# The first expert's tokens made by TensorE from the rows in SBUF, instead of gathered from DRAM

## The reference

```python
x = x + gate1 * ((sig(gA) * A @ w_pa + sig(gB) * B @ w_pb) @ w_o)
h = rmsnorm_mod(x, norm2_g, sh2, sc2)
# top-1 of 4 groups, then top-2 of its 4 experts, per token
y = sum over experts e of combine[:, e] * ((silu(h @ w_gate[e]) * (h @ w_up[e])) @ w_down[e])
x = x + gate2 * y
```

## Time and profile before

| | us |
|---|---|
| median of 3 runs | 1282.19 (1280.95 to 1283.69) |
| the profiled execution, its own time | 1284.0 |
| its span, first to last instruction | 1282.3 |
| mean granted TensorE clock | 0.984 |
| busy: PE, DVE, ACT, POOL | 1213.0, 666.9, 541.0, 200.3 |

### The profile page before, as it was taken

How to read it: one execution, slowest core, us unless ns; L and a number is a source line. 1 busy time by engine, 2 the same in 40 slices (tenths; PEclk the granted TensorE clock), 3 DMA queues, 4 the chain that set the end, 5 groups by cost and what they waited for, 6 DMA issues and landing times.

```text
span 1282.3 us, 17725 instructions
## 1 busy us (share of the span) xinstructions
PE 1213.0 (95%) x7058; PEld 923.6 (72%) x7058; DVE 666.9 (52%) x903; ACT 541.0 (42%) x850; POOL 200.3 (16%) x230
## 2 busy tenths in 40 slices
PE   4999999999999999998899999999999999999986
PEld 2677877777777987896766666657667887777762
DVE  2428433222162213213577641354777988888867
ACT  4533322111273135216333332121547777877742
POOL 2113200020000010002200021000163222323230
PEclk9999999999999999998899999999989999999999
DMA  9653222274534452557799995621689999999963
GB/s 335 245 214 108 81 66 66 66 240 146 215 117 130 172 208 105 180 190 263 274 347 384 380 332 193 203 107 33 218 278 321 378 373 375 370 373 378 372 229 119
DMA packets 128922, 294.47 MB, mean 230 GB/s; under 512 B 10016, under 2 KB 10144, under 8 KB 125080
## 3 DMA queue, kind: packets, MB, share of 16 engines
q1 hardware_dynamic: 111112, 243.57, 54.0%
q0 software_dynamic: 17744, 49.96, 11.0%
HBM read 270.44 MB, written 30.42 MB: 235 GB/s over the span
## 4 chain that ended last, share of the span: by engine, by line
PE 67%; DMA 19%; issue 4%; ACT 3%; DVE 3%; POOL 3%; POOLq 1%; SPq 0%; ACTq 0%; DVEq 0%
PE psum L1040 14%; PE psum L1042 14%; PE psum L1041 14%; DMA arena<-slots_d 9%; PE psum L1028 5%; PE psum L1102 5%; DMA arena<-in_cache_kv_w_dram 5%; DMA arena<-h2d,arena 3%; PE psum L1449 2%; PE psum L1283 2%; PE psum L1356 2%; PE psum L1055 1%; POOL slots_d L958 1%; POOL arena L977 1%; ACT arena L1665 1%
## 5 line engine op out<-in xcount | busy, mean ns | idle before, releaser
L1040 PE MATMUL psum<-part,part 128*128 128x512 f32 (+1 forms) x1088 | 437.0, 402 | 6.0 <-DVE part L2545 2.3
L1041 PE MATMUL psum<-part,part 128*128 128x512 f32 (+1 forms) x1088 | 428.9, 394 | 0.0
L1042 PE MATMUL psum<-part,part 128*128 128x512 f32 (+1 forms) x1088 | 428.6, 394 | 0.0
L1040 PEld LDWEIGHTS psum<-part,part 128*128 128x128 f32 (+1 forms) x1088 | 219.4, 202 | 61.2 <-issue 13.7
L1042 PEld LDWEIGHTS psum<-part,part 128*128 128x128 f32 (+1 forms) x1088 | 219.4, 202 | 42.6
L1041 PEld LDWEIGHTS psum<-part,part 128*128 128x128 f32 (+1 forms) x1088 | 219.6, 202 | 38.5
L2505 DVE TENSOR_TENSOR part<-arena,part 128x2048 fp32r<-128x2048 f32 x96 | 218.3, 2290 | 34.1 <-ACT part L1900 32.6
L1900 ACT ACTIVATE part<-arena 128x2048 fp32r<-128x2048 f32 x94 | 178.7, 1918 | 36.1 <-DMA arena<-in_w_down_dram 16.4
L1665 ACT ACTIVATE arena<-psum 128x512 f32<-128x512 f32 (+4 forms) x127 | 73.4, 598 | 273.0 <-PE psum L1042 223.3
L1999 DVE TENSOR_TENSOR part<-arena,part 128x2048 fp32r<-128x2048 f32 x42 | 96.0, 2299 | 141.4 <-PE psum L1102 118.3
L1028 PE MATMUL psum<-cst,arena 128*128 128x128 f32 (+2 forms) x746 | 103.8, 285 | 30.5 <-ACT arena L1693 9.7
(11 more groups left out here) (308 smaller groups left out, 1105.0 us busy)
## 6 DMA issues: line engine op xcount, KB each, us to landing
arena<-in_w_in_dram SPq DMA_DIRECT2D x34, 1024.0 KB, 5.4
arena<-in_cache_kv_w_dram SPq DMA_DIRECT2D x16, 2048.0 KB, 12.2
arena<-in_w_gate_dram SPq DMA_DIRECT2D x32, 1024.0 KB, 9.7
arena<-in_w_up_dram SPq DMA_DIRECT2D x32, 1024.0 KB, 8.9
arena<-in_w_down_dram SPq DMA_DIRECT2D x32, 1024.0 KB, 10.2
arena<-in_w_ada_dram SPq DMA_DIRECT2D x8, 2048.0 KB, 7.7
arena<-in_cache_kv_w_dram SPq DMA_DIRECT2D x16, 1024.0 KB, 9.7
arena<-in_w_ada_dram SPq DMA_DIRECT2D x8, 1024.0 KB, 14.4
```

Source lines behind the costliest of these rows:

```text
L1040: nc.tensor.matmul(out_, hi, w_hi, start=start, stop=False)
L1041: nc.tensor.matmul(out_, hi, w_lo, start=False, stop=False)
L1042: last_product[0] = nc.tensor.matmul(out_, lo, w_hi, start=False, stop=stop)
```

## The change

The gather of expert 0's tokens goes. PE makes them, already turned, into the same banks 0 and 1: for each block of 128 columns of h, the sum over the five tiles of `hrow`'s block (as weights) with `hot[0]`'s tile. POOL gathers for experts 1 and 2 only. `hot[0]` and `xg` lie elsewhere, since `hrow` must now stay until the products are made; SP's second `ahead` load waits for them (`x_filled` 2) too. The orders on PE, ACT and DVE around the change are written anew, and the six keep-warm products that PE makes behind the bank "pos" (two, three and one) go; the six in front of it stay.

```diff
-        hot = [kept[:, a:a + TILES * P].rearrange("p (i n) -> p i n", i=TILES) for a in (0, 3072, 1200)]
+        hot = [[gt_tmp[:, i * P:(i + 1) * P] for i in range(4)] + [at(KEPT0 + 6 * CH + D + 1100, P)]] + [
+            [kept[:, a + i * P:a + (i + 1) * P] for i in range(TILES)] for a in (3072, 1200)]
...
-        xg = at(TAIL0, 2, D)
+        xg = [at(TAIL0 + D, D), at(TAIL0, D)]
...
             sp.wait_ge(h2_out, 16 * TILES)
+            sp.wait_ge(x_filled, 2)
             sp.dma_start(ahead[1], gate1[:, 4:8, :]).then_inc(ahead_in[1], 16)
-            for par in range(2):
-                sp.wait_ge(xg_in[par], 16)
+            sp.wait_ge(xg_in[1], 16)
...
             pool.wait_ge(h2_out, 16 * TILES)
-            for e in range(3):
-                pool.wait_ge(slot_ready, e + 1)
+            pool.dma_start(yd[2 * TOK + 2:2 * TOK + 3, :], h2d[2:3, :]).then_inc(xg_in[0], 16)
+            for e in (1, 2):
+                pool.wait_ge(slot_ready, e)
                 if e == 2:
                     pool.wait_ge(x_filled, 2)
...
             mm.wait_emptied(pe, len(mm.users) - 1)
-            keep_warm(2)
-            for e in range(3):
+            tp.wait_emptied(pe, len(tp.users) - 1)
+            def place_of_slots(e):
                 pe.wait_ge(hot_done, e + 1)
                 for i in range(TILES):
-                    ins = nc.tensor.matmul(psum[:, 2 + e, 0:1], hot[e][0:ROWS[i], i, :], tok_left[0:ROWS[i], i:i + 1],
+                    ins = nc.tensor.matmul(psum[:, 2 + e, 0:1], hot[e][i][0:ROWS[i], :], tok_left[0:ROWS[i], i:i + 1],
                                            start=(i == 0), stop=(i == TILES - 1))
                 ins.then_inc(hot_filled, 1)
-            keep_warm(3)
+            pe.wait_ge(hot_done, 1)
+            for c in range(2):
+                for k in range(4):
+                    if c == 0 and k == 2:
+                        place_of_slots(1)
+                    for i in range(TILES):
+                        n, f = ROWS[i], (4 * c + k) * P
+                        ins = nc.tensor.matmul(psum[:, c, k * P:(k + 1) * P], hrow[0:n, i, f:f + P], hot[0][i][0:n, :],
+                                               start=(i == 0), stop=(i == TILES - 1))
+                ins.then_inc(x_filled, 1)
+            place_of_slots(2)
...
             prime(pe, 1, up_read, up_filled, y0_filled, y1_filled)
-            for c in range(2):
-                turn_tokens(0, 0, 0, c)
-            keep_warm(1)
             pe.wait_ge(x_lo, 1)
...
-            for at_ in range(2, 4):
-                high(at_, 16)
+            high(2, 16)
+            tokens_high(0, 0, 0)
+            high(3, 16)
+            tokens_high(0, 0, 1)
             rounds = rounds_of(act)
-            for c in range(2):
-                tokens_high(0, 0, c)
+            act.wait_ge(h2_out, 16 * TILES)
             silu(0)
...
-            slots_of(0)
+            slots_of(1)
+            low(0, 7)
+            tokens_low(0, 0, 0)
+            low(1, 8)
             compared(2)
-            low(0, 7)
-            slots_of(1)
+            tokens_low(0, 0, 1)
             for k, mk in enumerate((m1, m2)):
...
             V.tensor_copy(row_u, rowf).then_inc(rows_done, 1)
             slots_of(2)
-            low(1, 8)
             rounds = rounds_of(dve)
...
-            for c in range(2):
-                tokens_low(0, 0, c)
             for at_ in range(2, 4):
                 low(at_, at_ + 7)
```

More of the change, by code:

```diff
@@ L947, in _ @@
             pool.wait_ge(h2_out, 16 * TILES)
-            for e in range(3):
-                pool.wait_ge(slot_ready, e + 1)
+            pool.dma_start(yd[2 * TOK + 2:2 * TOK + 3, :], h2d[2:3, :]).then_inc(xg_in[0], 16)
+            for e in (1, 2):
+                pool.wait_ge(slot_ready, e)
                 if e == 2:
                     pool.wait_ge(x_filled, 2)
-                pool.indirect_dma_start(xg[:, e % 2, :], None, h2d, bass.IndirectOffsetOnAxis(
+                pool.indirect_dma_start(xg[e % 2], None, h2d, bass.IndirectOffsetOnAxis(
                     ap=slot_hot[:, e:e + 1], axis=0), bounds_check=TOK - 1, oob_is_err=False).then_inc(xg_in[e % 2], 16)
@@ L976, in fetch @@
                 waited()
-                pool.indirect_dma_start(xg[:, par, :], None, h2d, bass.IndirectOffsetOnAxis(
+                pool.indirect_dma_start(xg[par], None, h2d, bass.IndirectOffsetOnAxis(
                     ap=slot_u[:, par, 0:1], axis=0), bounds_check=TOK - 1, oob_is_err=False).then_inc(xg_in[par], 16)
@@ L1567, in turn_tokens @@
                     pe.wait_ge(xg_in[par], it * 16 + 16)
-                if not isinstance(n, int) or n > 0:
-                    pe.wait_ge(x_lo, n * 2 + c - 1)
+                pe.wait_ge(x_lo, n * 2 + c - 1)
                 for k in range(4):
                     ins = nc.tensor.transpose(X[c][:, k * P:(k + 1) * P],
-                                              xg[:, par, (4 * c + k) * P:(4 * c + k + 1) * P], ident)
+                                              xg[par][:, (4 * c + k) * P:(4 * c + k + 1) * P], ident)
                 ins.then_inc(x_filled, 1)
@@ L2490, in compared @@
                 for i in range(TILES):
-                    ins = V.tensor_scalar(hot[e][:, i, :], c_("iota"), 1.0, nth[:, i, e:e + 1], ALU.add, ALU.is_equal)
+                    ins = V.tensor_scalar(hot[e][i], c_("iota"), 1.0, nth[:, i, e:e + 1], ALU.add, ALU.is_equal)
                 ins.then_inc(hot_done, 1)
             def slots_of(e):
-                dve.wait_ge(hot_filled, e + 1)
+                dve.wait_ge(hot_filled, e)
                 own(V.tensor_scalar(slot_f[:, e:e + 1], psum[:, 2 + e, 0:1], -1.0, float(TOK), ALU.mult, ALU.add))
@@ L2516, in _, with tokens_low @@
             V.tensor_copy(rounds_u, rounds_f).then_inc(tp_dve, 1)
-            slots_of(0)
+            slots_of(1)
+            def tokens_low(par, n, c):
+                dve.wait_ge(x_hi, n * 2 + c + 1)
+                V.tensor_tensor(xgT_lo[:, par, 4 * c:4 * c + 4, :], psum[:, c, :].rearrange("p (k n) -> p k n", k=4),
+                                xgT[:, par, 4 * c:4 * c + 4, :], ALU.subtract).then_inc(x_lo, 1)
+            low(0, 7)
+            tokens_low(0, 0, 0)
+            low(1, 8)
             compared(2)
-            low(0, 7)
-            slots_of(1)
+            tokens_low(0, 0, 1)
             for k, mk in enumerate((m1, m2)):
```

## The result

The kernel with the change takes 1292.74 us (median of 4 runs, 1292.27 to 1297.05), the one before on the same chip 1281.57 (1279.77 to 1283.69): ratio 1.0107, 95% interval 1.0083 to 1.0131. It is slower, by 11.2 us where 6.9 were forecast, 0.2 us above the range. The profiled execution is the slowest of the four: 1297.05 us, span 1295.4.

The account below looks back on a forecast made before the run. The prediction took POOL's queue (third gather, ten scatters, yd store) to set the time in this stage. Its terms 5.1 + 1.3 + 0 + 0.5 = 6.9 us on 1282.2 gave 1289.1 us, range 1284.0 to 1292.5.

Parts of the forecast that it names:

- Part 1: On PE, the first gather goes and 40 f32 products (80 instructions) replace it, starting at 930.95 after DVE's `rounds_u`.
- Part 2: Price of PE's products: 0.106 us per instruction at full clock, first 20 at half clock, `x_filled` 2 at 942.9.
- the array stays at 1.2 GHz: Rival: PE at half clock through all products, `x_filled` 2 at 950.4, third gather +12.6, 1296 us; chance 0.06.
- Part 3: DVE's order: `slots_of(2)` comes last in a row, at 947.35, so POOL's third gather starts at 948.15, +5.1 us.
- Part 4: POOL: third gather's call lengthened by DVE's `low(2)`, +1.3 us; ten scatter calls 0, with -2 to +2; stores 0.
- Part 5: Hidden loads: SP's second `ahead` load and expert 1's gather move later but land before they are needed.
- Part 6: PE's restart after idling some 8 us instead of 2.3: a longer half-clock stretch, 0 to 1.6 us more, taken as +0.5.
- Nothing given back: Later in the kernel, PE runs without a gap and POOL's chain shifts alike, so 0 us of the delay is recovered.
- only PE's path counts: Rival: POOL's chain doesn't bind, only the later first expert product costs, +1.2, 1283.4 us; within 0.2% had chance 0.12.
- POOL free of DVE: Rival: third gather takes 0.99 and ten calls 12.7 us, PE's gap closes, about 1279.3 us; chance 0.04.

Follow-up runs that it names:

- a_warm: Changed kernel with four keep-warm products where PE waits for the release of "pos": 1291.69 us, ratio 1.0096.
- a_all: Changed kernel with four keep-warm products, 128 rows for the fifth tile, early row numbers, and POOL's scatters ahead of its wait for expert 2's slots: 1279.06 us, ratio 0.9998.
- a_poolfirst: Changed kernel with DVE's row numbers right behind `rounds_u` and the ten scatters ahead of the third gather, behind the wait for expert 2's slots: 1286.01 us, ratio 1.0050.
- a_pad: Changed kernel with the fifth tile's products run over all 128 rows instead of 64: 1286.94 us, ratio 1.0051.
- b_dve_order: Kernel before, gather kept, with DVE's row numbers, weights and `slots_of(2)` moved behind both `tokens_low` of expert 0: 1286.09 us, ratio 1.0052.
- a_same: The changed kernel run again, unaltered: 1294.01 us, ratio 1.0123 to the kernel before.
- b_late_pe: Kernel before with seven more keep-warm products ahead of PE's first expert product: 1283.31 us, ratio 1.0023.
- b_scatter_first: Kernel before with POOL's ten scatters ahead of the gather for expert 2 and its slot wait, DVE's order kept: 1278.46 us, ratio 0.9980.
- a_ydearly: Changed kernel with POOL's two stores to yd moved from behind the scatters to ahead of the gathers: 1293.74 us, ratio 1.0101.
- a_scatter_first: Changed kernel with row numbers right behind `rounds_u` and the ten scatters also ahead of the wait for expert 2's slots: 1286.79 us, ratio 1.0046.

## Why the prediction was right in sign and low in size

Counted from R, in the profiled executions (forecast, then measured):

| step | forecast | measured |
|---|---|---|
| last product (`x_filled` 2) | 12.0 | 18.5 |
| from there to the third gather | 5.25 | 5.4 |
| third gather against before | +5.1 | +11.7 |
| its call | +1.3 | 0.0 |
| ten calls with gaps, 20.0 before | 0 | +3.3 |
| yd store, 5.28 before | 0 | +0.6 |
| from yd to PE's restart | 0 | 0.0 |
| PE at the restart | | +15.6 |
| half clock after the restart | +0.5 | up to 0.8 |
| given back by the end | 0 | -2.4 |
| end | +6.9 | +14.0 |

- *Part 1* was right: PE starts at 930.08, 0.11 us after R.
- *Part 2*, the price of the products, is the step that failed. It took 18.4 us and not 11.9, and the whole error of the third gather (6.6 us) is in it. The mechanism that the prediction named, PE's products holding up DVE's row and through it POOL, was the one that ran; this term of its sum was too small. "The nearest row has the same shape" was not true: L1217 has no 64-row tile. The edges of the fifth tile cost 3.1 us of the 80 instructions at full clock (a_warm's 13.5 against a_all's 10.4, placing included). The clock costs 1.6 with one fall and 5.0 with two; I had reckoned 2.1. So of the 6.5 us, 3.1 are the edges, 2.9 the clock, and the last 0.5 is mostly the step of 0.112 where I took 0.106. A second fall under busy products was in no case of mine. My rival "the array stays at 1.2 GHz" had the price (19.4) with one long stretch as its mechanism; after didn't run so, but a_poolfirst nearly did (half clock until 942), and 0.06 was too little for it. The row that could have warned me was in the trace: the twenty one-column products took 0.13 us each at full clock, more than the 0.106 of a product 128 times as wide, and they have the fifth tile too (ten of them take 1.36 us in a_warm, 1.17 in a_pad).
- *Part 3* was right: with `x_filled` 2 put right, DVE's order gives the third gather to 0.2 us, and b_dve_order shows the mechanism by itself.
- *Part 4*: the gather's call took 1.03 us, not 2.3. DVE's `low(2)` began at 953.85 and the call at 953.86: a call that begins with a subtraction needn't be held up, one that begins under it is. The ten calls took 23.3 us, beyond my ±2, since eight of them were held up and not six. The term of 0 had assumed that as many subtractions give as many long calls; what counts is where the calls begin.
- *Part 5* was right: no wait on the ahead load or expert 1's gather is in the chain.
- *Part 6*: the restart is at 0.50 until 994 and 0.56 on average from 994 to 996, some 5 us against 3.6 before; up to 0.8 us.
- *The range*: its upper end took 1 us for the calls where Part 4 allowed 2. With 2 the sum at the bounds is +11.1, 1293.3, and the measured median would have lain inside it, with Part 2 as wrong as it is. That the calls' 3.3 and the products' 6.5 were partly set off by the gather's 1.3 and by 2.4 at the end is luck.
- *Nothing given back* held through the loop (PE's restart is 15.6 us late, the last turn 16.5). Behind it 2.5 us are gone: from the last turn to the end after takes 70.0 us and before 72.5. The other kernels take 69.7 to 71.5 there, so it is before's own profiled execution (1284.0, above all the other runs listed for it) that stands out; that the change gives anything back isn't shown.
- The profiled executions differ by 13.1 us, the medians by 11.2, since after was profiled in its slowest run, with two falls of the clock. a_same, with one fall, took 1292.74 in its profile, which is after's median, by chance.

Of the rivals, "only PE's path counts" fell with b_dve_order, though b_late_pe shows that path to cost too once its 2.3 us are used up. "POOL free of DVE" happened in b_late_pe (eight calls alone), but not in the changed kernel. What stays open: why the clock falls a second time, or stays down longer, in some executions and not in others.

## What to carry to other kernels

Price a product by a row with the same row counts, not only the same columns, and pad a short last tile when it stands among full ones. When a wait is moved, follow every way from the late engine to the bound one (here yd to `result`, and the scatters to `fetch` and the gather): taking one away shows only the next. Compare the starts of POOL's calls with DVE's subtractions, and not only their numbers. Here a late turn of expert 3 was as late at the last turn (after 16.4 and 16.5 us, b_late_pe 1.6 and 1.8), while an early one lost part of its lead (b_scatter_first 4.3 and 2.5, a_all 3.3 and 2.9).

## What the runs showed of the hardware that was not expected

- Among 128-row f32 products at full clock, each change of the row count, to 64 and back, put two steps of 0.20 to 0.21 us in place of 0.11 (a_warm: 60 in 9.09 us; padded to 128 rows: 60 in 6.95).
- The granted clock fell from 1.00 to 0.50 in the midst of products that kept PE busy (after, 938 to 944) in one execution and not in another of the same kernel (a_same, 934 to 944 at 1.00); it fell so in a_ydearly and a_scatter_first too.
- An indirect call on POOL that began under a 128x2048 subtraction of DVE ended 0.77 to 0.96 us after it (94 calls in 14 profiles); one that began before the subtraction kept its 0.90 to 1.05 us. Ten indirect stores took from 14.7 to 23.3 us with gaps, by how many began so.
